# Rotary turns on VectorE: rows swapped by a shuffle, scores that wait per head, and turns at other steps

## What is computed

```python
def apply_rope(x, cs):
    cos, sin = cs
    xf = x.astype(jnp.float32).reshape(x.shape[:-1] + (x.shape[-1] // 2, 2))
    x1, x2 = xf[..., 0], xf[..., 1]
    c = cos[None, :, None, :]
    s = sin[None, :, None, :]
    out = jnp.stack([x1 * c - x2 * s, x1 * s + x2 * c], axis=-1).reshape(x.shape)
    return out.astype(x.dtype)

def mixing_sublayer(h, p, layer, ctx, rope):
    da_q, da_k, da_v, m_q, m_kv, m_kr, s_q, s_k, s_v = jnp.split(h @ p['w_in'], offs, axis=-1)
    ...
    q1, q2 = apply_rope(q1, rope64), apply_rope(q2, rope64)              # DA: 4 heads, two maps each
    k_lat = jnp.concatenate([apply_rope(k_own[..., :DA_DH], rope64),
                             apply_rope(k_own[..., DA_DH:], rope64)], axis=-1)
    ...
    q_rope = apply_rope(q_rope, rope32)                                  # MLA: 8 heads, 32 of 96 rows
    kr_lat = apply_rope(kr_own[:, :, None, :], rope32)[:, :, 0]
    ...
    window_attention(apply_rope(q_s, rope64), apply_rope(k_s, rope64), ...)   # SWA: 8 heads on 2 key heads
```

## Time and profile before

| | us |
|---|---|
| median of 3 runs | 3224.54 (3221.62 to 3229.37) |
| the profiled execution | 3220.77 |
| its span, first to last instruction | 3219.0 |
| its mean granted PE clock | 0.952 of full speed |

### The profile page before, as it was taken

The page is one execution under the profiler, slowest core; times in us unless marked ns, Lnnn a source line. Parts: engine busy times, 40 slices in busy tenths (PEclk is TensorE's granted clock), DMA queues, the critical chain, the costliest instruction groups (busy, mean ns, idle before and its releaser), DMA issues.

```text
span 3219.0 us, 45689 instructions
## 1 busy us (share of the span) xinstructions
PE 2895.4 (90%) x16160; PEld 2267.4 (70%) x16160; DVE 2013.1 (63%) x3162; ACT 1636.8 (51%) x2385; POOL 230.1 (7%) x278
## 2 busy tenths in 40 slices
PE   6979988988988999999988798889799799999996
PEld 3758955877976767776656696569598577767774
DVE  3363245355357999999835523443744699999995
ACT  3152334234236777777633523341432477777774
POOL 0050012011000000000002300110200000000000
PEclk9989999999988999999998899999999699999997
DMA  7202100210358999999811021012023399999992
GB/s 279 72 14 87 56 28 27 80 68 27 138 185 313 343 334 332 338 338 336 302 69 59 27 91 54 1 53 93 29 92 145 144 349 333 331 339 338 332 349 84
DMA packets 280125, 564.24 MB, mean 175 GB/s; under 512 B 14040, under 2 KB 19872, under 8 KB 279328
## 3 DMA queue, kind: packets, MB, share of 16 engines
q1 hardware_dynamic: 273056, 543.33, 47.1%
q10 hardware_dynamic: 4448, 9.87, 0.8%
q0 software_dynamic: 2464, 8.91, 0.7%
HBM read 546.44 MB, written 15.63 MB: 175 GB/s over the span
## 4 chain that ended last, share of the span: by engine, by line
PE 67%; DVE 16%; issue 6%; ACT 5%; ACTq 2%; DVEq 2%; DMA 1%; POOL 0%; POOLq 0%; SPq 0%
PE mm L989 22%; PE mm L1492 18%; DVE w_lo L2055 7%; PE mm L1002 5%; PE mm L1234 2%; PE mm L1030 2%; DVE x L2063 2%; ACTq L1983 2%; DVE scratch L2055 2%; PE oo L1256 1%; ACT w_hi L1570 1%; DVE scratch L2274 1%; ACT scratch L1570 1%; PE oo L960 1%; PE tp L1243 1%
## 5 line engine op out<-in xcount | busy, mean ns | idle before, releaser
L2055 DVE TENSOR_TENSOR w_lo<-ring,w_hi 128x1024 fp32r<-128x1024 f32 x768 | 912.1, 1219 | 102.6 <-ACT w_hi L1570 86.7
L1570 ACT ACTIVATE w_hi<-ring 128x1024 fp32r<-128x1024 f32 x768 | 803.4, 1059 | 278.4 <-PE mm L1492 256.2
L2055 DVE TENSOR_TENSOR ring_lo<-ring,dw_hi 128x512 fp32r<-128x512 f32 x200 | 135.9, 684 | 431.8 <-ACT dw_hi L1570 431.5
L1570 ACT ACTIVATE dw_hi<-ring 128x512 fp32r<-128x512 f32 x200 | 123.9, 624 | 477.9 <-PE mm L989 473.4
L989 PE MATMUL mm<-h_hi,ring_lo 128*128 128x320 f32 (+1 forms) x1344 | 316.9, 318 | 18.6 <-DVE ring_lo L2055 12.5
L989 PE MATMUL mm<-h_lo,dw_hi 128*128 128x320 f32 (+1 forms) x1344 | 310.5, 313 | 0.0
L989 PE MATMUL mm<-h_hi,dw_hi 128*128 128x320 f32 (+1 forms) x1344 | 309.4, 312 | 0.0
L989 PEld LDWEIGHTS mm<-h_hi,ring_lo 128*128 128x128 f32 (+1 forms) x1344 | 225.6, 190 | 42.2 <-issue 28.2
L989 PEld LDWEIGHTS mm<-h_lo,dw_hi 128*128 128x128 f32 (+1 forms) x1344 | 227.4, 190 | 1.2
L989 PEld LDWEIGHTS mm<-h_hi,dw_hi 128*128 128x128 f32 (+1 forms) x1344 | 226.4, 189 | 1.2
L1492 PE MATMUL mm<-w_lo,xa_hi 128*80 128x512 f32 x512 | 204.6, 400 | 23.6 <-DVE w_lo L2055 11.8
(11 more groups left out here) (301 smaller groups left out, 5421.2 us busy)
## 6 DMA issues: line engine op xcount, KB each, us to landing
ring<-in_w_ff SPq DMA_DIRECT2D x384, 1024.0 KB, 6.6
ring<-in_w_ada SPq DMA_DIRECT2D x48, 1024.0 KB, 7.4
ring<-in_w_gate SPq DMA_DIRECT2D x24, 1024.0 KB, 5.8
ring<-in_w_in SPq DMA_DIRECT2D x16, 1024.0 KB, 9.4
ring<-in_w_o SPq DMA_DIRECT2D x8, 1024.0 KB, 8.2
x_spill<-x SPq DMA_DIRECT2D x2, 2560.0 KB, 13.0
ring<-in_w_br_da SPq DMA_DIRECT2D x4, 1024.0 KB, 6.2
ring<-in_w_br_mla SPq DMA_DIRECT2D x4, 1024.0 KB, 6.2
```

The costliest lines, as they stand in the source:

```text
L1570: return act.activation(out, in_, ACT.Copy, scale=scale)
L2055: return dve.tensor_tensor(out, in0, in1, op)
```

## The change

All swap products are gone, with the constants `swap` and `swap32`; the sign of the swap is in the sine tables. `rope` now shuffles the tile's rows into a temporary with DVE's `stream_shuffle` (the same permutation of 32 rows in each group of 32), multiplies the tile by the cosines, drains, multiplies the temporary by the signed sines, drains, and adds: four operations, all on SBUF. The buffer counts lose these turns: MLA's head takes seven `mm` turns in place of eight.

DA: each tile is turned on DVE after it has been copied, `da_roped` counts tiles, and a score of the first four steps waits for its own head's key tile alone. The last key tile is turned between the maxima of step 0 and the reciprocals of step 1; the transposes of new keys stand behind score 0. MLA: the three parts of a head's turn are at t = 2 (shuffle and cosines, at the step's end), t = 3 (sines, at the end) and t = 4 (add, ahead of the maximum). SWA: the four query tiles are turned in `merge` of the MLA branch, at m = 1..4 (`beside`), and only the key tile after it.

The core of the diff:

```diff
@@ PE, DA
-                    pe.matmul(mm[j % 2][:, 0:NLAT], c_("swap"), src, start=True, stop=True).then_inc(mm_full[j % 2], 1)
-                for q in range(4):
+                for q in range(8):
                     product_h(l, q, (lambda k: pe.wait_ge(h_lo_ready, l * KT + (k + 1))) if q == 0 else None)
-                for m in range(4):
-                    da_rotate(m)
-                    product_h(l, H_AT["da_k"] + m)
-                for m in range(4, 8):
-                    da_rotate(m)
-
-                wait_t_empty(pe, l, TR["da_new"])
-                for m in range(4):
-                    last = pe.transpose(tp[:, m * P:(m + 1) * P], da_k[:, m, T:KEYS], ident)
-                last.then_inc(t_full, 1)
-                pe.wait_ge(da_roped, l + 1)
...
+                    if t == 0:
+                        pe.wait_ge(da_roped, l * 8 + 4 + hd + 1)
...
+                    if s == 0:
+                        da_new_keys()
@@ PE, MLA
-                    else:
-                        pe.matmul(mm[j % 2][MNOPE:MQ, 0:NLAT], c_("swap32", slice(MNOPE, MQ)),
-                                  ml_q[hd % 2][MNOPE:MQ, 0:NLAT], start=True, stop=True).then_inc(mm_full[j % 2], 1)
...
-                    if 1 <= t <= 3 and hd < MH - 1:
+                    if 1 <= t <= 2 and hd < MH - 1:
                         project_head(hd + 1, t - 1)
@@ PE, SWA
                 for q in range(2):
-                    sw_rotate(2 * q)
-                    sw_rotate(2 * q + 1)
                     product_h(l, H_AT["sw_kv"] + q)
-                sw_rotate(4)
@@ DVE, rope
-            def rope(l, j, dst, rows_, cos, sin, t_):
-
-                wait_mm_full(dve, l, j)
-                tt(t_[rows_, 0:NLAT], mm[j % 2][rows_, 0:NLAT], sin, ALU.mult).then_inc(mm_empty[j % 2], 1)
+            def rope(dst, rows_, cos, sin, t_):
+
+                dve.stream_shuffle(t_[rows_, 0:NLAT], dst, SWAP)
                 tt(dst, dst, cos, ALU.mult)
+                dve.drain()
+                tt(t_[rows_, 0:NLAT], t_[rows_, 0:NLAT], sin, ALU.mult)
                 dve.drain()
                 return tt(dst, dst, t_[rows_, 0:NLAT], ALU.add)
@@ DVE, DA
+                for m in range(7):
+                    lo_of_tile(l, m + 1)
+                    da_rope(m)
...
+                    if s == 0:
+                        da_rope(7)
@@ DVE, MLA
+                    if t == 4 and hd < MH - 1:
+                        rope_head(hd + 1, 2)
                     if s < MLA_N:
...
                     if 2 <= s < MLA_N + 2 and (s - 2) % TT in (1, 3):
                         mla_turn_odd(s - 2)
+                    if t in (2, 3) and hd < MH - 1:
+                        rope_head(hd + 1, t - 2)
@@ DVE, SWA
-                merge(l, 1, MM["mla_out"], False, H_AT["mla_gate"])
+                merge(l, 1, MM["mla_out"], False, H_AT["mla_gate"], beside=sw_q_rope)
...
+                wait_mm_read(dve, l, SW_K)
+                rope(sw_kraw[:, 0:NLAT], slice(0, P), c_("cos64"), c_("sin64"), tmp[0])
```

More of the change, by code:

```diff
@@ L252 @@
 MLA_NORM = [MM["mla_in"] + n for n in (5, 7)]
[L256 to L259 removed]
+DA_K = [MM["da_k"] + m for m in range(4)]
+SW_K, SW_V = MM["sw_kv"], MM["sw_kv"] + 1
+SWAP = [p ^ 1 for p in range(32)]
 H_TILES, H_AT = [], {}
@@ L2147, in lo_of_merged, with merge @@
                 tt(mg_lo[:, k, :], merged[:, k, :], mg_hi[:, k, :].bitcast(FP32), ALU.subtract).then_inc(mg_ready, 1)
-            def merge(l, g, turn, first, q0, turned=None):
+            def merge(l, g, turn, first, q0, turned=None, beside=None):
                 _, _, _, kept = ada_plan(l, g)
@@ L2163, in merge @@
                         turned()
+                    if beside is not None:
+                        beside(m)
                     wait_mm_read(dve, l, turn + 2 * m)
```

103 lines of the change are left out of this document (38 added, 65 removed).

## The result

The changed kernel takes 3137.22 us (median of 4 runs, 3136.78 to 3137.75), the kernel before 3223.55 us in the same session (3221.62 to 3229.37). The ratio is 0.973, with a 95% interval of 0.971 to 0.975: 86 us less. The forecast was 3137, the range 3118 to 3160.

What follows compares the result with a forecast made beforehand. PE, busy for 90% of the span, was taken to bound the kernel. Gains of 38.9 us a layer, 77.8 in all, and 10 of clock took 3220.8 to 3133.0; the median, 3.8 above, was forecast at 3137, range 3118 to 3160.

Steps and rivals of the forecast that it cites:

- The price of a turn: On DVE: shuffle 0.61, cosines 0.75, sines 0.75 and add 0.69, 2.8 us in place of 2.05; the shuffle taken as 0.69 long.
- DA's input tiles: DA: four tiles without a swap product take 7.04 us rather than 8.61, 6.4 us a layer; seven turns covered between subtractions.
- the way to the scores: DA, last tile to scores: first maximum gains 9.1 us, the last key's turn loses 0.7; together 8.4 us a layer.
- rival (d): DA: the scores still wait for all turns; it would cost 17 us, 3154; chance 0.01.
- MLA's heads: A head takes 15.7 us rather than 17.64, 2.0 less (swap product 1.0, wait 1.0); seven heads give 14.0 a layer.
- SWA: From the branch's last product to the first scores 17.0 us rather than 25.2, gain 8.2 a layer; query turns cost nothing.
- The clock: PE's lower clock ahead of DA, MLA and SWA scores: filled idle stretches give 10 us of some 17 in both layers.
- the 3 us at DA: Estimate of what a layer loses at DA to PE's lower clock.
- sum of 77.8: Gains of 6.4, 8.4, 1.9, 14.0 and 8.2, 38.9 us a layer, 77.8 in both, without the 10 us of clock.
- Rival (c): PE's clock falls to 1.2 GHz in MLA's heads; gain lost at 6 of 14, 3251 at eight; chance 0.03.
- Rival (b): MLA's head finds another wait, only the swap product's 1.0 us goes; 14 us less gain, 3151; chance 0.09.
- Rival (a): The shuffle is dear, nine a layer on the path: at 1.22 us 3146, at 2.5 us 3170; chance 0.08.

## Why the prediction was right, and where its reasons were not

**The price of a turn** held: 0.63 from shuffle to cosines, 2.8 for the turn. Not foreseen was the mask load ahead of each shuffle, 0.01 us as a row and at most 0.1 as a gap. The Trainium skill's rate (VectorE: DVE Perf Modes, the perf-mode tier table), a quarter of 2400 ns, gave an estimate of 0.6; the start-to-start time agrees with it, the row's duration of 0.73 is above.

**DA's input tiles and the way to the scores** held: the key tiles' subtractions start 7.04 us apart (127.97, 135.01, 142.05), the first maximum is 2.3 us behind the last tile, maximum 1 another 5.1. That the seven turns are covered was shown by doubling and by leaving out. But **rival (d)** was priced wrongly, at the whole 8.4 us a layer; awaiting all turns costs 3.0 in both layers together (3.7 against a kernel of the same session). The 8.4 belong to the turns' place between the tiles, not to the wait.

**MLA's heads**: 15.94 rather than 15.7. The step that was off put idle time at two waits, 1.3 us; there are three, 1.56. The step that failed is the split behind it, "Of the 2.0 the swap product is 1.0 ... and the wait gives 1.0". The two are not terms that can be added, and that the head met its total does not bear them out. The four kernels with the shuffle's turn, heads from the second on:

| the turn stands | product on PE | no product on PE |
|---|---|---|
| in t = 3, ahead of the copy | 19.5 us, total 3185.3 | 20.4 us, total 3204.9 |
| spread over t = 2, 3, 4 | 16.52 us, total 3150.2 | 15.94 us, total 3137.2 |

Removing the product costs 0.9 a head in the first row and gives 0.6 in the second; the move is worth 3.0 or 4.5. Against the 17.64 of the earlier trace rows, whose turn is three operations with the first ahead of the maximum and no longer than 2.05 us, the exchange without the move is a loss of 2.8 (of about 2 against the averages of 18.1 and 18.6). The total came out right because the change does both.

**SWA** held to 0.1 us. With the four query turns behind the merge, the same stretch takes 19.8 us rather than 17.0, so the moved turns, which I counted as free, are also what makes the 8.2 possible: 2.8 of it. There the second tile's subtraction comes 1.30 us late for PE, and PE waits 1.18 us more for the key copies.

**The clock**: I took 10 us; the ledger gives 11. The 8.4 us at DA had already counted score 0 at the higher clock, 1.1 us a layer, and the 3 us at DA in the paragraph on the clock may hold it again, so up to 12 us of the forecast are clock. With the 0.24 us of the longer head taken off fourteen times, the forecast's sum of 77.8 is 74.4, and the rest of the 84.0 is 9.6. Where it sits I had partly wrong: DA's score 2 still runs at the lower clock, and most of the gain is in the heads.

**Two small errors cancelled.** The profiled execution was to take 3133.0 us and took 3136.8; the median was to lie 3.8 us above it and lies 0.4 above. That the median was met to 0.2 us is luck; the forecast gain of 87.8 us in the profiled execution was 84.0, with the head's 0.24 us as the largest part of the difference.

**Rival (c)** had 0.03 and a break-even at 6 of 14 heads. For the changed order it was wrong, as the reason against it said (PE's busy share in a head is 0.90). But it describes the nearest neighbour of this kernel: with the turn in its old step the heads lose clock, about 2.4 us each rather than the 14.3 I priced. Together with the longer waits the gain shrinks from 86 to 17 us. I should have asked how much longer PE's wait may be before it comes in, and given the case more weight: the margin was the place of one copy. **Rival (b)**, another wait in the head, came true in its mildest form, 0.24 us a head. **Rival (a)** fell with the shuffle's row.

**What stays open.** What exactly makes the clock fall was not measured. The runs show heads with 1.6 us of idle time at 1.00, with 2.5 (before) at 0.96, with 3.2 at 0.94 and with 3.6 at 0.83, but the same waits in the same kernel come out either way, in the first heads and with the doubled shuffles. The opposite half of the change, the copy ahead of the turn with the swap products kept and no shuffle, was not run, so how much of the 86 us the order alone would give is not known; the changed kernel with the product put back, at 3150, only comes near it for MLA.

## What to carry to other kernels

Work that is taken off the bounding engine is a gain only if the engine that takes it over has it done before anyone waits; here the exchange alone was worth 0 us of 86, and the same exchange with its operations in idle stretches of VectorE all of them. Look for the instruction that is awaited (here a 0.82 us copy) and keep the new work behind it, not ahead. When a change leaves the matrix engine both less to do and a longer wait, price the wait with its clock too: here the values behind it took 2.40 us rather than 1.31, in every turn of the loop.

## What the runs showed of the hardware

- A shuffle of 512 four-byte columns takes 0.72 us on 32 partitions (723 ns) and 0.74 on 128 (737 ns), with the next operation 0.61 to 0.63 us after its start where no drain stands between; each comes with a mask load, a row of 0.01 us.
- More work on PE made a kernel 20 us faster (3204.9 to 3185.3), with the granted clock at 0.94 rather than 0.83 over 80 us of heads.
- Before the change the next head's first score ran at the full clock (1.25 us) in 9 of 14 heads behind a wait of 2.47 us. A wait of 3.04 us without the swap product had values of 2.40 us behind it in all 14; with a product back they took 1.31 to 1.40 in 8 of 14, although the wait was 3.23.
- One wait does not settle the clock: behind 1.25 us the same values took 1.31 and 2.35 us in two heads of one kernel.
